# Layer norm of the Conformer block: group sums with z as moving operand, statistics in all partitions, and products that keep TensorE occupied in two waits

## What is computed

```python
def layer_norm(x, g, b):
    mu = jnp.mean(x, axis=-1, keepdims=True)
    xc = x - mu
    var = jnp.mean(xc * xc, axis=-1, keepdims=True)
    return xc * lax.rsqrt(var + LN_EPS) * g + b

def conformer_conv_module(h, w_pw1, b_pw1, w_dw, b_dw, ln_g, ln_b, w_pw2, b_pw2):
    a = h @ w_pw1 + b_pw1
    u = a[..., :CONV_CH] * jax.nn.sigmoid(a[..., CONV_CH:])
    y = causal depthwise convolution of u, width 31, + b_dw
    y = jax.nn.silu(layer_norm(y, ln_g, ln_b))
    return y @ w_pw2 + b_pw2
```

## Time and profile before

| | us |
|---|---|
| median of 3 runs | 1764.96 (1763.54 to 1765.1) |
| the profiled execution, its own time | 1765.51 |
| the profiled execution, span of its trace | 1763.7 |
| TensorE busy | 1751.2 (99%), 12753 products |
| VectorE busy | 1330.7 (75%) |
| ScalarE busy | 832.4 (47%) |
| memory traffic | 102 GB/s over the span |

### The profile page before, as it was taken

The page is one execution under the profiler, slowest core; times in us unless marked ns, Lnnn a source line. Parts: engine busy times, 40 slices in busy tenths (PEclk is TensorE's granted clock), DMA queues, the critical chain, the costliest instruction groups (busy, mean ns, idle before and its releaser), DMA issues.

```text
span 1763.7 us, 31054 instructions
## 1 busy us (share of the span) xinstructions
PE 1751.2 (99%) x12753; PEld 1571.5 (89%) x12753; DVE 1330.7 (75%) x1918; ACT 832.4 (47%) x1389; POOL 31.2 (2%) x63
## 2 busy tenths in 40 slices
PE   9999999999999999999999999999999999999999
PEld 7899899887588899899988998999887988998998
DVE  6899488589758897497588974966887788974964
ACT  5446255355835455255354552553424554552652
POOL 0000000032000000000000000000000000000000
PEclk9999999999999999999999999999998999999999
DMA  6333223322032333223223332332454223322331
GB/s 203 108 131 109 96 98 115 123 67 81 2 108 69 115 116 108 96 99 118 96 72 119 109 107 96 108 119 85 123 167 126 97 75 116 119 97 96 110 107 49
DMA packets 74438, 183.22 MB, mean 104 GB/s; under 512 B 23712, under 2 KB 30512, under 8 KB 74304
## 3 DMA queue, kind: packets, MB, share of 16 engines
q1 hardware_dynamic: 72128, 179.02, 30.7%
q0 software_dynamic: 1600, 1.52, 0.3%
q10 hardware_dynamic: 576, 0.79, 0.1%
HBM read 174.35 MB, written 6.29 MB: 102 GB/s over the span
## 4 chain that ended last, share of the span: by engine, by line
PE 97%; DVE 1%; DMA 1%; issue 0%; ACT 0%; SPq 0%; ACTq 0%; DVEq 0%
PE bank L866 36%; PE bank L525 16%; PE bank L526 16%; PE bank L527 16%; PE bank L618 4%; PE bank L623 2%; PE bank L927 1%; PE bank L959 1%; PE bank L1025 1%; PE bank L903 1%; PE bank L552 1%; PE bank L544 1%; PE bank L942 1%; PE bank L922 0%; PE bank L592 0%
## 5 line engine op out<-in xcount | busy, mean ns | idle before, releaser
L525 PE MATMUL bank<-a_hi,w_hi 128*128 128x512 f32 (+1 forms) x912 | 334.8, 367 | 1.1 <-issue 1.1
L526 PE MATMUL bank<-a_lo,w_hi 128*128 128x512 f32 (+1 forms) x912 | 332.9, 365 | 0.0
L527 PE MATMUL bank<-a_hi,w_lo 128*128 128x512 f32 (+1 forms) x912 | 332.7, 365 | 0.0
L1170 ACT ACTIVATE w_hi<-w_raw 128x1024 fp32r<-128x1024 f32 x192 | 202.7, 1058 | 198.4 <-DVE w_raw L1550 160.1
L866 PE MATMUL bank<-x_hi,w_hi 128*128 128x256 f32 x1024 | 290.1, 283 | 0.0
L866 PE MATMUL bank<-x_lo,w_hi 128*128 128x256 f32 x1024 | 289.7, 283 | 0.0
L866 PE MATMUL bank<-x_hi,w_lo 128*128 128x256 f32 x1024 | 289.6, 283 | 0.0
L1542 DVE TENSOR_TENSOR w_lo<-w_raw,w_hi 128x1024 fp32r<-128x1024 f32 x192 | 234.5, 1222 | 27.3 <-ACT w_hi L1170 26.4
L1530 DVE TENSOR_TENSOR w_lo<-w_raw,w_hi 128x1024 fp32r<-128x1024 f32 x142 | 173.6, 1223 | 90.7 <-ACT w_hi L1119 90.3
L1119 ACT ACTIVATE w_hi<-w_raw 128x1024 fp32r<-128x1024 f32 x142 | 146.6, 1052 | 198.1 <-PE bank L527 185.4
L866 PE MATMUL bank<-raw_forms_hi,w_lo 128*128 128x256 f32 x768 | 215.8, 281 | 0.0
(11 more groups left out here) (245 smaller groups left out, 2919.6 us busy)
## 6 DMA issues: line engine op xcount, KB each, us to landing
w_raw<-stream SPq DMA_DIRECT2D x312, 512.0 KB, 3.2
h_resid<-xT SPq DMA_DIRECT2D x8, 256.0 KB, 6.2
qT<-stream SPq DMA_DIRECT2D x8, 256.0 KB, 6.2
u_scratch<-V SPq DMA_DIRECT2D x8, 256.0 KB, 2.4
a_lo<-u_scratch SPq DMA_DIRECT2D x8, 256.0 KB, 3.0
qT<-z_scratch SPq DMA_DIRECT2D x8, 256.0 KB, 4.4
outT<-h_resid SPq DMA_DIRECT2D x10, 128.0 KB, 1.8
z_scratch<-kT SPq DMA_DIRECT2D x2, 256.0 KB, 4.6
```

Of the source, the lines that this page charges most:

```text
L525: nc.tensor.matmul(out, lw[0], lx[0], start=first, stop=False)
L526: nc.tensor.matmul(out, lw[0], lx[1], start=False, stop=False)
L527: return nc.tensor.matmul(out, lw[1], lx[0], start=False, stop=last)
L1170: nc.scalar.activation(units_to(w_hi, pair, split), units_from(pair, split), ACT.Copy).then_inc(s_uhi, 1)
```

## The change

The sums over groups are turned round: same_q, all 128 columns, is the stationary operand and z, 64 columns of one group, the moving one. There are 8 products for a sum and not 16, each with the whole array, and the result stands in every partition for its phase, 64 columns wide. dl, dl_sq and var are therefore 128x64 tiles and take the room of the early sums. `broadcast_phases` turns round too: a column of the identity, repeated, is stationary and picks the partition of a phase; the statistics move. `keep_busy` adds 10 products with constants between the halves of convolve(6) and 14 after it, into the upper half of bank 4; the wait for s_root goes ahead of them. ScalarE writes a_hi by a Silu straight from y and then f by a second Silu, without the copy. VectorE's `next_slot` for a pw2 slot moves from before dl to after the first normalised chunk, and the low part of chunk 0 comes between the two steps of chunk 1.

```diff
--- before.py
+++ after.py
@@ -214,9 +214,9 @@
                U[:, 1, :], u[0], G[:, 1, :])]
         zsq_sum, *zsq = [z.rearrange("p (g n) -> p g n", g=GROUPS) for z in (G[:, 0, :], U[:, 0, :], ss[:, :])]
         m0 = sb("mean_early", [P, NT])
-        dl, dl_sq, var = sb("mean_rest", [P, PH]), sb("mean_rest_sq", [P, PH]), sb("var", [P, PH])
+        early = sq[:, 0, :].rearrange("p (j n) -> p j n", n=NT)
+        dl, dl_sq, var = (early[:, j, :] for j in range(EARLY))
         std = var
-        early = sq[:, 0, :].rearrange("p (j n) -> p j n", n=NT)
         rest = sq[:, 1, :].rearrange("p (g n) -> p g n", g=GROUPS)
         mats = [room[:, i * MAT:(i + 1) * MAT]
                 for room, first, count in ((spare, 0, 1), (more, 0, 2), (fv, 0, 1), (yv, 0, Y_MATS), (fv, 1, 5))
@@ -1031,11 +1031,14 @@
                 def sum_groups(out, src, first, last):
 
                     for g in range(GROUPS):
-                        for part in range(2):
-                            ins = nc.tensor.matmul(out[part * NT:(part + 1) * NT, 0:PH], src[:, g, :], same_q[:, 0:PH],
-                                                   start=(first and g == 0), stop=(last and g == GROUPS - 1),
-                                                   skip_group_check=True)
+                        ins = nc.tensor.matmul(out[:, 0:NT], same_q, src[:, g, :], start=(first and g == 0),
+                                               stop=(last and g == GROUPS - 1), skip_group_check=True)
                     return ins
+
+                def keep_busy(count):
+
+                    for _ in range(count):
+                        nc.tensor.matmul(bank[4][:, T // 2:T], ident_b[:, :], mask[:, 0, :], start=True, stop=True)
 
                 def sum_centred(j):
                     pe.wait_ge(s_zc, j + 1)
@@ -1065,13 +1068,16 @@
                 body(n0 + 14, 2)
                 convolve(EARLY + 1, A)
                 body(n0 + 15, 3, lambda: convolve(EARLY + 1, B))
-                for i in range(EARLY + 2, CONVS - 1):
-                    convolve(i)
+                convolve(EARLY + 2)
+                convolve(EARLY + 3, A)
+                pe.wait_ge(s_root, 3 * sub + 1)
+                keep_busy(10)
+                convolve(EARLY + 3, B)
+                keep_busy(14)
                 pe.wait_ge(s_m0, 1)
                 pe.wait_ge(s_rest, 3)
                 sum_groups(BCAST, rest, True, False)
                 convolve(CONVS - 1)
-                pe.wait_ge(s_root, 3 * sub + 1)
                 pe.wait_ge(s_zsqadd, CONVS - 2)
                 sum_groups(STAT, zsq_sum, True, False)
                 sum_centred(7).then_inc(s_dlmm, 1)
@@ -1081,9 +1087,8 @@
             def broadcast_phases(out, v):
 
                 for q in range(PH):
-                    at = slice(q % 2 * NT, (q % 2 + 1) * NT)
                     ins = nc.tensor.matmul(out[:, q % 2, q // 2 * NT:(q // 2 + 1) * NT],
-                                           v[at, q:q + 1].broadcast_to([NT, P]), ident[at, at], start=True, stop=True)
+                                           ident[:, q:q + 1].broadcast_to([P, P]), v, start=True, stop=True)
                 return ins
 
             def layer_norm():
@@ -1472,15 +1477,15 @@
                 for i in range(EARLY + 2, CONVS):
                     square(i)
                 act.wait_ge(s_var, 1)
-                nc.scalar.activation(std[:, :], var[:, :], ACT.Sqrt, bias=eps[:, 1:2]).then_inc(s_lroot, 1)
+                nc.scalar.activation(std, var, ACT.Sqrt, bias=eps[:, 1:2]).then_inc(s_lroot, 1)
                 nc.scalar.activation(tiny[:, 1:2], eps[:, 0:1], ACT.Silu)
                 for m in range(KD):
                     act.wait_ge(s_z, m + 1)
 
+                    nc.scalar.activation(a_hi[:, m, :], y[:, m, :], ACT.Silu,
+                                         bias=col("ln_b", m), scale=col("ln_g", m)).then_inc(s_zhi, 1)
                     nc.scalar.activation(f[:, m, :], y[:, m, :], ACT.Silu,
                                          bias=col("ln_b", m), scale=col("ln_g", m)).then_inc(s_zact, 1)
-                    act.wait_ge(s_zact, m + 1)
-                    nc.scalar.activation(a_hi[:, m, :], f[:, m, :], ACT.Copy).then_inc(s_zhi, 1)
 
             act.wait_ge(s_ones, 1)
             sqrt_table()
@@ -2078,18 +2083,17 @@
                 for i in range(3, CONVS - 1):
                     add_squares(i)
                 centred(7)
-                next_slot(n, n % RING)
 
                 dve.wait_ge(s_dlmm, 1)
-                nc.vector.tensor_scalar(dl[:, :], BCAST[:, 0:PH], 1.0 / D, None, ALU.mult).then_inc(s_dl, 1)
+                nc.vector.tensor_scalar(dl, BCAST[:, 0:NT], 1.0 / D, None, ALU.mult).then_inc(s_dl, 1)
                 dve.wait_ge(s_dl, 1)
-                link(nc.vector.tensor_tensor(dl_sq[:, :], dl[:, :], dl[:, :], ALU.mult))
+                link(nc.vector.tensor_tensor(dl_sq, dl, dl, ALU.mult))
                 dve.wait_ge(s_sqmm, 1)
-                link(nc.vector.scalar_tensor_tensor(out=var[:, :], in0=STAT[:, 0:PH], scalar=1.0 / D, in1=dl_sq[:, :],
+                link(nc.vector.scalar_tensor_tensor(out=var, in0=STAT[:, 0:NT], scalar=1.0 / D, in1=dl_sq,
                                                     op0=ALU.mult, op1=ALU.subtract))
-                nc.vector.tensor_scalar(var[:, :], var[:, :], 0.0, None, ALU.max).then_inc(s_var, 1)
+                nc.vector.tensor_scalar(var, var, 0.0, None, ALU.max).then_inc(s_var, 1)
                 dve.wait_ge(s_lroot, 1)
-                nc.vector.reciprocal(std[:, :], std[:, :]).then_inc(s_linv, 1)
+                nc.vector.reciprocal(std, std).then_inc(s_linv, 1)
                 for m in range(KD):
                     dve.wait_ge(s_y[m], 16)
                     if m == 0:
@@ -2098,13 +2102,18 @@
                     link(nc.vector.tensor_tensor(z, z, phases(3), ALU.subtract))
                     if m == 0:
                         dve.wait_ge(s_lbc, 2)
+                    if m == 1:
+                        z_lo_of(0)
                     nc.vector.tensor_tensor(z, z, phases(2), ALU.mult).then_inc(s_z, 1)
-                    if m:
+                    if m == 0:
+                        next_slot(n, n % RING)
+                    if m > 1:
                         z_lo_of(m - 1)
                 z_lo_of(KD - 1)
 
             def z_lo_of(m):
                 dve.wait_ge(s_zhi, m + 1)
+                dve.wait_ge(s_zact, m + 1)
                 nc.vector.tensor_tensor(a_lo[:, m, :], f[:, m, :], a_hi[:, m, :].bitcast(F32), ALU.subtract
                                         ).then_inc(s_zlo, 1)
```

## The result

The changed kernel takes 1766.64 us (median of 22 runs) and the kernel before 1763.91 us (22 runs): a ratio of 1.0023, with a 95% interval of 1.0016 to 1.003. It is slower, by little: the forecast of no change and its sign were wrong, though 1766.64 lies inside the range. The prediction took 0.2% for the least that a measurement can tell; this one tells 0.07% to either side, so 2.7 us stand clear of the noise. Four of the 22 executions took 1773.5 to 1774.9 us at a mean granted clock of 0.994 or 0.995, where the other 18 took 1765.0 to 1769.0 at 0.998 to 1.000; the ratio holds these four, and the medians differ by 2.7 us. Without them the mean of after is 1766.5 us, still slower.

A forecast was written before the change was run, and what follows sets the result against it. TensorE bounds the kernel (97% of the span). Pw2 start +0.05, its first block's clock -1.05, block 1 +0.3, y6 +0.4 make -0.3: 1765.2 against 1765.51, median 1764.7 us; range 1760.6 to 1769.2.

The forecast's parts named there:

- y6 late: End of pw2: y6, queued behind the moved weight split, lands late and makes TensorE wait 0.4 us.
- my -0.3: Whole kernel: the summed terms give -0.3 us against the profiled execution's 1765.51 us, in short no change.
- A group sum: Sums over groups: 16 wide records at 0.10 us each, so 1.6 us a sum against 1.0 before at full clock.
- The 0.107 us that stands beside my value: Group sums: the skill page's load time, columns / 1.2, estimates 0.107 us at either clock.
- Rival 2: Sums and broadcasts: records at 0.055, clock held, fetches early; 3.5 us faster, 1761.2 us; chance 0.2.
- the quicker: Conv 7: the next instruction piece comes 3.55 us after entry at 1341.15, so at 1344.7; with 4.0 at 1345.15.
- the full clock gains nothing here: Conv 7: the instruction stall takes the full clock's gain; it ends at 1345.3 against 1345.18 before.
- rival 1: Statistics: the clock still falls, costing +1.7 to 7.5 us, middle +4, 1768.7 us; chance 0.25.
- The 35 records at half clock: Rival 1's threshold in the statistics: from 35 records at half clock (3.5 us) the sign turns.
- The copy's -0.65: Before pw2: Silu straight into the high part removes ScalarE's copy, 0.68, say -0.65 us.
- 2.73 + 0.3: Pw2's first block: 2.73 us at full clock, then a 0.3 us stall because the moved weight split delays block 1.
- rival 3: Last block of pw2: late y6 and the split bind it, 1 us more, 1765.7; shorter a_hi path brings nothing; chance 0.08.

The follow-up runs named there:

- the halves of the rows: The changed kernel with broadcast products using 64 of the 128 partitions, lower and upper in turns; 1765.78 us, ratio to before 1.0015.
- the shorter ones: The changed kernel with its 24 keep-busy products of 256 columns cut into 48 of 128 columns; 1767.09 us, ratio to before 1.0013.
- wide sums alone: The kernel before with only the turned sums, turned broadcasts and 128x64 statistics; 1767.03 us, ratio to before 1.0023.
- the narrow-sum kernel: The changed kernel with the sums, 128x8 statistics and broadcasts of the kernel before put back; 1767.77 us, ratio to before 1.0018.
- 32 short fillers, pairs and halves: The kernel before with paired-group sums, half-row broadcasts, direct Silu, 32 products of 64 columns after conv 6, five of 256 between broadcasts; 1761.93 us, ratio 0.9995.

## Why the prediction was wrong, by its own steps

Counted from conv 5's start in both kernels:

| step | predicted | measured | error |
|---|---|---|---|
| start of the first sum | 9.41 | 9.96 | +0.55 |
| its length | 1.6 | 1.90 | +0.30 |
| conv 7's end | 14.76 | 16.12 | +1.36, the two above in it |
| three sums | 4.8 | 5.41 | +0.61 |
| two broadcasts | 3.2 | 3.80 | +0.60 |
| to pw2's first product | 1.85 | 1.64 | -0.21 |
| to its third block | 5.76 | 5.94 | +0.18 |
| y6 late | 0.4 | 0 | -0.4 |

The errors add to 1.36 + 0.61 + 0.60 - 0.21 + 0.18 - 0.4 = 2.14 us, which turns my -0.3 into the +1.84 measured between the two traces. No mechanism that I named was missing. Four terms were too small (the first sum's start, the price of a record in sums and broadcasts, the fetch in conv 7, the first two blocks of pw2), and the two that were too large give back only 0.6.

**The record (step "A group sum").** This is the step that failed most. I took 0.10 us from six records of the early sum. Over the three sums it is 5.41 / 48 = 0.113, start to start, and the steps from the first sum to conv 7 and from the broadcasts to the next form cost 0.1 and 0.2 more (1.90 and 3.80 against 16 and 32 times 0.113). With the first sum's 0.30, the three sums' 0.61 and the broadcasts' 0.60 this is 1.5 us, the largest part of the error. 0.12 was my upper bound; by it the sum would have come out at 1.9 us more. The value that I took came from a row too short to give a rate, and I did not read the loads of those six records. In the trace of before they are

```profile
1307.38 0.86 PEld L1048 LDWEIGHTS bank<-sq_tmp,conv_consts 128*128 128x128 f32 x6
```

They start 0.22 us ahead of the first product (1307.60), while a product of 512 columns still runs, and lie (0.86 - 0.19) / 5 = 0.13 us apart; the row of products hides the first of them. The 0.107 us that stands beside my value in the prediction was nearer to the 0.113 measured. Rival 2 (0.055 by overlapping loads) did not happen in this form, but the halves of the rows show that it is to be had: (1.11 - 0.27) / 15 = 0.056.

**Conv 6 and the ten products.** Half a microsecond (0.55): conv 6's stall was 0.13 us longer, and from its end to the first sum it was 1339.97 - 1335.30 = 4.67 us, where I had 1339.95 - 1335.70 = 4.25. Of these 0.42 us, 0.30 lie in conv 6 itself, 2.90 us with the ten products in it where I had 2.6, again without the steps from one form to the next. I had the ten products' 1.2 us in the sum; without the ten, conv 7 ends 2.5 us earlier in the trace, and the median is 2.15 us lower.

**Conv 7's instructions.** Place and cause were right: record 123, 1.46 us (predicted 1 to 1.5), with the clock full. The piece was entered 0.7 us late, for the two reasons above, and the successor came 4.1 us after, where I took "the quicker" 3.55 out of 3.5 and 4.0. These 0.7 and 0.55 us and 0.1 in the 37 records behind the stall make the 1.36. Counted in the same way it is 2.4 us (without the ten products) to 5.1 us (with the shorter ones) over the experiments. That conv 7 ends as early at the partly halved clock without keep-busy products (14.98) as with wide sums alone at the full one (14.94) fits the sentence that "the full clock gains nothing here".

**The clock, rival 1.** The profiled execution kept 1.00, as forecast. Rival 1 was priced at up to 7.5 us, and 4 of 22 executions are 6.9 to 8.3 us above the median of the others at a mean clock of 0.994 or 0.995: 0.005 of 1772 us is 9 us of full speed lost, or 18 us at half clock, which is about from the statistics to pw2's first block. I have no trace of such an execution, so the match is in size only. (The 35 records at half clock that were to turn the sign are those that make 3.5 us; against a forecast of -0.3, three already cancel it.) The same happened in 2 of 12 executions with wide sums alone and in 1 of 12 with halves of the rows. The forecast should have named it as something that happens in part of the executions rather than as one of two outcomes.

**Statistics of 64 columns.** The scaling took 0.23 as expected, but the reciprocal 0.55 us and not the 0.25 that I took for each step. It cost nothing because the mean's broadcast, 1.9 us long, hid it; with short broadcasts it is what TensorE waits for.

**Silu, pw2, y6.** The copy's -0.65 came as -0.66 (2.25 to 1.59 us from the multiplication on), but only because the clock was full; at half clock it is 0.26. From pw2's first product to the next block it took 3.06 us where I had 2.73 + 0.3. The size was right by luck: the largest part of what the two blocks lose comes from the order of VectorE's steps (0.30 us) and little from the split (0.07), to which I had given all of it, and I had no loss in the second block (0.15). y6 went out at 1363.69 us, some 1.5 later than computed (the split ended later), but landed within 3.0 us where I had 4.4, so at about 1366.6 as computed. VectorE wanted it only at 1367.17, not at 1364.9, mostly because its first chunk was 1.8 late, and kept its pace of 1.92 us for a chunk. There is no part of rival 3 in the time.

**The reference point.** I set the result against the one profiled execution and took off 0.55 us, its distance to the median of three runs. Its span of 1763.7 us is 1.5 above the median span of before's, 1762.2, and its interval of 31.07 was longer than the only other one (30.05). So of the median's +2.7 us the two traces show 1.84, and nearly one was already in what I compared with.

What stays open: why the clock falls in some executions of after and not in others, what makes the fetch take 2.4 us once and 5.1 us another time, and how much of the loss of the narrow-sum kernel is its stall and how much its clock.

## What to carry to other kernels

A turned product that halves the records but fills the array with each weight load is no gain: price it by the load (0.113 us for 128 columns here), take fewer and longer products, and let neighbours use different halves of the rows. Where a row of tiny products outruns the fetch of its own instructions, a faster clock or a shorter stage before it comes back as stall, so work is to be taken from behind the stall, and filler products belong only where the engine waits for another engine. A rate from six records whose first load is hidden under the product before them is not a price: read the loads' own row as well. And a step from one form of work to the next costs 0.1 to 0.2 us that a sum of rates forgets.

## What the runs showed of the hardware that was not expected

- Weight loads of 128 fp32 columns, back to back over the same rows, follow each other by 0.113 us at the full clock; with neighbours on different halves of the rows 16 records take 1.11 instead of 1.95 us. Moving columns under them are nearly free up to 128: a record of 64 or of 128 takes 0.11 to 0.13.
- With wide sums alone and no filler the clock stayed at 1.00 in the trace over two pauses of 1.7 us, and its mean was 0.998 or more in 10 of 12 executions; without the keep-busy products of after it fell in conv 7 (0.66) and was full again in the wide sums. With narrow sums it fell although 24 fillers ran (0.59, 0.50, 0.54). With 32 short fillers, pairs and halves the mean was 0.999 or 1.000 in all eleven executions.
- A stall for instructions is 0.2 to 2.3 us and sits where 128 records since the last piece are used up; it moves by exactly the number of records that are added ahead of it or left out. In conv 7 it was at record 131 in before, 123 in after, 99, 107 and 133 with more or fewer products ahead, 147 and 155 without the keep-busy ones.
- The Trainium skill ("Runtime: NRT & Kernel Launch", Instruction fetch mechanics) has pieces of 256 instructions, with which the stall's moves from record 123 to 99 and 107 agree; that such a fetch is mostly hidden does not hold for this kernel's convolutions: conv 6 and conv 7 stall for 1.56 and 0.57 us in before and for 1.69 and 1.46 in after.
- The reciprocal of 128x64 took 0.55 us on VectorE, where the scaling of the same size took 0.23.
